# Six weight differences of each head on GpSimd, and VectorE's SBUF-SBUF operations in the three-operand form

## The reference

```
h    = rmsnorm(x, pre_w) * (1 + scale) + shift
proj = h @ w_in                              # q, k, v, z, b, a, rx, gate
# DeltaNet head: short conv, silu, l2norm; then per chunk and direction
tmat = strict_lower((k*beta) @ k.T * decay) + I
u, w = solve(tmat, [v*beta, k*beta*exp(g)])
v_new = u - w @ S;  o = (q*exp(g)) @ S + (q @ k.T * decay) @ v_new
S = S * gl + (k*exp(g_last - g)).T @ v_new
# RG-LRU block: gates r, i from x; a = exp(-8 r softplus(-lam))
h_t = a_t * h_{t-1} + sqrt(1 - a_t**2) * i_t * x_t      # both directions
y = x + gate * rmsnorm(concat(o * silu(z), h * silu(gate)) @ w_out, post_w)
```

## Time and profile before

| | |
|---|---|
| median of three runs | 1477.31 us (1476.23 to 1486.73) |
| the profiled execution | 1494.5 us |
| its span | 1492.9 us |
| mean granted clock of TensorE | 0.954 |
| busy: TensorE, VectorE, ScalarE, GpSimd | 1404.3, 1017.6, 751.4, 118.5 us |
| VectorE's differences of `w_in` (L1449) | 51, 68.2 us |
| heads 1 to 7 start their scans near | 374, 514, 653, 794, 933, 1077, 1219 us |

### The profile page before, as it was taken

One profiled execution on the slowest core, in us unless ns is written; L12 is line 12 of the kernel. 1 busy time (PEld: TensorE's weight loads), 2 busy tenths in 40 slices (PEclk: granted clock), 3 DMA queues, 4 the chain that ended last, 5 costly groups with the idle time before them and its releaser, 6 DMA issues.

```text
span 1492.9 us, 24459 instructions
## 1 busy us (share of the span) xinstructions
PE 1404.3 (94%) x8198; PEld 1256.5 (84%) x8198; DVE 1017.6 (68%) x2101; ACT 751.4 (50%) x1878; POOL 118.5 (8%) x144
## 2 busy tenths in 40 slices
PE   6899999999999899989999998999999987699997
PEld 3599989987998799889989997998899864488886
DVE  4775867786778778777976797878678845722222
ACT  3535474646465655666474647465646644411110
POOL 3001000100010000000000100010001000211211
PEclk9999989996999999999989999999699978699999
DMA  8221111111012111111111102012102350432440
GB/s 322 71 70 42 29 38 52 45 47 56 19 45 64 43 30 61 34 43 45 45 34 58 45 31 72 19 48 61 43 16 74 129 218 32 141 103 88 126 126 29
DMA packets 95203, 100.48 MB, mean 67 GB/s; under 512 B 4293, under 2 KB 81350, under 8 KB 94058
## 3 DMA queue, kind: packets, MB, share of 16 engines
q1 hardware_dynamic: 92138, 88.38, 19.2%
q0 software_dynamic: 2944, 10.49, 1.8%
HBM read 83.55 MB, written 15.30 MB: 66 GB/s over the span
## 4 chain that ended last, share of the span: by engine, by line
PE 83%; ACT 7%; issue 4%; DVE 4%; DMA 1%; SPq 0%; DVEq 0%; ACTq 0%
PE bank L722 14%; PE bank L720 14%; PE bank L721 14%; PE bank L1025 13%; PE bank L888 4%; PE bank L932 3%; PE bank L977 2%; PE bank L848 2%; PE bank L995 2%; PE bank L987 2%; PE bank L968 2%; PE bank L963 2%; PE bank L810 2%; ACT L1178 1%; PE bank L899 1%
## 5 line engine op out<-in xcount | busy, mean ns | idle before, releaser
L720 PE MATMUL bank<-hT_hi,w_hi 128*128 128x384 f32 (+1 forms) x1224 | 439.2, 359 | 3.4 <-DVE hT_lo L1477 3.4
L722 PE MATMUL bank<-hT_hi,w_lo 128*128 128x384 f32 (+1 forms) x1224 | 417.1, 341 | 0.0
L721 PE MATMUL bank<-hT_lo,w_hi 128*128 128x384 f32 (+1 forms) x1224 | 416.4, 340 | 0.0
L720 PEld LDWEIGHTS bank<-hT_hi,w_hi 128*128 128x128 f32 x1224 | 233.3, 191 | 7.5 <-issue 3.2
L721 PEld LDWEIGHTS bank<-hT_lo,w_hi 128*128 128x128 f32 x1224 | 233.5, 191 | 1.2
L722 PEld LDWEIGHTS bank<-hT_hi,w_lo 128*128 128x128 f32 x1224 | 232.4, 190 | 0.0
L1314 ACT ACTIVATE arena<-bank,arena 128x128 f32<-128x128 f32 x272 | 78.6, 369 | 185.8 <-PE bank L977 185.6
L1533 DVE SCALAR_TENSOR_TENSOR arena<-arena 128x1154 f32<-128x1154 f32 x96 | 135.9, 1416 | 3.5 <-DVE arena L1531 1.1
L1025 PE MATMUL bank<-wo_hi,ot_hi 128*128 128x512 f32 x288 | 114.6, 398 | 17.5 <-DVE ot_lo L1851 13.4
L1025 PE MATMUL bank<-wo_lo,ot_hi 128*128 128x512 f32 x288 | 113.9, 396 | 0.0
L1025 PE MATMUL bank<-wo_hi,ot_lo 128*128 128x512 f32 x288 | 113.9, 395 | 0.0
(11 more groups left out here) (233 smaller groups left out, 2394.0 us busy)
## 6 DMA issues: line engine op xcount, KB each, us to landing
w_raw<-w_in SPq DMA_DIRECT2D x51, 512.0 KB, 4.0
arena<-scr_G SPq DMA_DIRECT2D x16, 576.0 KB, 4.9
ot<-scr_o SPq DMA_DIRECT2D x9, 1024.0 KB, 6.7
arena<-x_sample SPq DMA_DIRECT2D x16, 512.0 KB, 7.6
arena<-ada_w SPq DMA_DIRECT2D x8, 1024.0 KB, 17.0
wo<-w_out SPq DMA_DIRECT2D x4, 2048.0 KB, 22.4
scr_o<-arena POOLq DMA_DIRECT2D x8, 576.0 KB, 3.1
scr_o<-arena POOLq DMA_DIRECT2D x8, 512.0 KB, 2.9
```

What stands on the lines that cost most here:

```text
L720: pe.matmul(out, w_hi[:, slot, k], hT_hi[:, k, cols], start=first, stop=False)
L721: pe.matmul(out, w_hi[:, slot, k], hT_lo[:, k, cols], start=False, stop=False)
L722: return pe.matmul(out, w_lo[:, slot, k], hT_hi[:, k, cols], start=False, stop=last)
```

## The change

All six differences of a head leave VectorE's list and are put into GpSimd's, as the same subtraction with the same semaphore. The six of the prologue stay with VectorE. In GpSimd's list numbers 4 and 5 stand behind the clearing of Zt, before the store of the head's output; number 6 stands behind that store; number 1 stands at the head of the loop's body, before the store of the states; numbers 2 and 3 stand behind the masks. Apart from that, VectorE's `tensor_tensor` operations whose two operands both lie in SBUF (in `rg_piece`, `norm_o` and the elimination) become `scalar_tensor_tensor` with a factor of 1.0, which computes (a * 1.0) op b.

```diff
@@ GpSimd @@
+            def low_w(slot, made):
+                gp.wait_ge(w_hi_made.sem, made)
+                gp.tensor_tensor(w_lo[:, slot], w_raw[:, slot], w_hi[:, slot].bitcast(F32), ALU.subtract)\
+                  .then_inc(w_lo_made.sem, 1)
+
             def phase_a(b):
...
                 gp.wait_ge(decay_exped.sem, decay_exped.next(b, INST))
                 own(gp.tensor_tensor(clear_mark, ident[:, 0:1], ident[:, 0:1], ALU.mult))
                 gp.memset(Zt, 0.0).then_inc(Zt_cleared.sem, 1)
+                low_w(1, w_lo_made.at(b, 4))
+                low_w(0, w_lo_made.at(b, 5))
...
             masks(-1)
             phase_a(-1)
+            low_w(1, w_lo_made.at(-1, 6))
             own.clear()
             with gp.Fori(0, HEADS - 1) as h:
+                low_w(0, w_lo_made.at(h, 1))
                 stores(h)
                 masks(h)
+                low_w(1, w_lo_made.at(h, 2))
+                low_w(0, w_lo_made.at(h, 3))
                 gp.wait_ge(stepped.sem, stepped.at(h, 18))
...
                 store_rg(h)
                 phase_a(h)
                 store_oz(h)
+                low_w(1, w_lo_made.at(h, 6))
@@ VectorE: the same form in "sum", "gate" and norm_o @@
-                    dve.tensor_tensor(RB, RB, RC, ALU.mult).then_inc(rg_bx_made.sem, 1)
+                    dve.scalar_tensor_tensor(RB, RB, 1.0, RC, ALU.mult, ALU.mult).then_inc(rg_bx_made.sem, 1)
@@ VectorE: phase_a @@
-                low_w(1, w_lo_made.at(b, 4))
                 own.settle()
...
-                low_w(0, w_lo_made.at(b, 5))
...
-                    if k == 10:
-                        low_w(1, w_lo_made.at(b, 6))
...
-                    own(dve.tensor_tensor(tmp, X[:, k + 1:, k:k + 1].to_broadcast([P, rows, k]),
-                                          X[:, k:k + 1, 0:k].to_broadcast([P, rows, k]), ALU.mult))
-                    own(dve.tensor_tensor(X[:, k + 1:, 0:k], X[:, k + 1:, 0:k], tmp, ALU.add))
+                    own(dve.scalar_tensor_tensor(tmp, X[:, k + 1:, k:k + 1].to_broadcast([P, rows, k]), 1.0,
+                                                 X[:, k:k + 1, 0:k].to_broadcast([P, rows, k]), ALU.mult, ALU.mult))
+                    own(dve.scalar_tensor_tensor(X[:, k + 1:, 0:k], X[:, k + 1:, 0:k], 1.0, tmp, ALU.mult, ALU.add))
@@ VectorE: joins and scan @@
-                    if slot == 10:
-                        low_w(0, w_lo_made.at(b, 1))
...
-                        if step == 1:
-                            low_w(1, w_lo_made.at(b, 2))
-                        if step == 7:
-                            low_w(0, w_lo_made.at(b, 3))
```

More of the change, by code:

```diff
@@ L1601, in rg_piece @@
                     dve.wait_ge(rg_scanned.sem, rg_scanned.at(b, 6))
-                    dve.tensor_tensor(RH, RH, RC, ALU.add).then_inc(rg_out_made.sem, 1)
+                    dve.scalar_tensor_tensor(RH, RH, 1.0, RC, ALU.mult, ALU.add).then_inc(rg_out_made.sem, 1)
                 else:
@@ L1605, in rg_piece @@
                     dve.wait_ge(silued.sem, silued.at(b, 2))
-                    dve.tensor_tensor(RH, RH, sg, ALU.mult).then_inc(rg_out_made.sem, 1)
+                    dve.scalar_tensor_tensor(RH, RH, 1.0, sg, ALU.mult, ALU.mult).then_inc(rg_out_made.sem, 1)
             def norm_o(b):
@@ L1610, in norm_o @@
                 own(dve.reciprocal(hcc["rstd"], hcc["rstd"]))
-                dve.tensor_tensor(o_tok, o_tok, hcc["rstd"].unsqueeze(2).to_broadcast([P, NCH, P]), ALU.mult)\
+                dve.scalar_tensor_tensor(o_tok, o_tok, 1.0, hcc["rstd"].unsqueeze(2).to_broadcast([P, NCH, P]), ALU.mult, ALU.mult)\
                    .then_inc(o_normed.sem, 1)
```

## The result

The changed kernel takes 1569.01 us (median of 4 runs, 1558.64 to 1570.97), the kernel before 1481.8 us beside it (4 runs, 1476.23 to 1486.73): ratio 1.0575, 95% interval 1.0507 to 1.0644, 87 us slower. The forecast was 1530 us with a range to 1552: the direction is right, the size is short by 39 us (52.7 us slower forecast, 87 measured). The profiled execution took 1567.3 us, span 1565.7 (before 1492.9), so the profiles differ by 72.8 us; before's own was 13 us above its median.

What follows compares the result with a forecast made beforehand. TensorE's projections were taken to set a head's length, VectorE ending slightly ahead. Stop 34.7, clock 16 and contention 2 sum to 52.7 us; added to the median 1477.3 this gave 1530 us, range 1504 to 1552.

Steps and rivals of the forecast that it cites:

- The stop at tile 3: TensorE waits at tile 3 for GpSimd's difference 4, behind the clearing: 4.4 us seven times, 3.9 once, 34.7 us.
- The clock behind the stops: After each TensorE stop the granted clock falls to half: 2.0 us times 8, 16 us, between 0 and 23.
- Rival (a): TensorE's stop at tile 3 alone, the clock does not fall for it: 1514 us, chance 0.26.
- Contention: GpSimd's differences hold VectorE's operations by the SBUF lock, mainly at the first convolution tap: 2 us, from 0 to 6.
- VectorE about 50 us less busy: Sign expected in the changed profile: VectorE about 50 us less busy, and idle longer before the joins.
- the elimination pairs at their old durations: Sign expected in the changed profile: VectorE's elimination pairs take as long as before.
- The form: VectorE's three-operand form costs the same as the two-operand one (1355 against 1361 ns at 128x1154): 0 us.
- Removed work: The differences leaving VectorE, 45 x 1.23 = 55 us less work there: a gain of 0, bound 8.6 us.
- Rival (b): GpSimd's difference 1 gets in between VectorE's two recurrence scans and holds the long one: 16 us more, 1546, chance 0.13.
- nothing downstream has time to give: the seam's slack is VectorE's, not TensorE's: Behind TensorE's stop every later reader follows TensorE; at the seam between heads VectorE idles 1.50 us before the joins.
- The range's upper end: 1552 us, from 40.7 for the stops, 23 for the clock, 6 for contention and 5 more: 75 us.

Runs made afterwards that it cites:

- e2: The kernel before with difference 4 alone moved to GpSimd, behind the clearing of Zt; VectorE waits for it before difference 5. Measured 1526.7 us, ratio 1.0319.
- e4: The changed kernel, but SyncE's load of the next head's tile 0 also waits for the head's last projection. Measured 1538.3 us, ratio 1.0417.
- e10: The changed kernel with difference 4 given back to VectorE at its old place. Measured 1479.7 us, ratio 1.0008.
- e1: The changed kernel; inside the loop GpSimd makes difference 4 before its wait for the decay's exponentials, prologue as in the change. Measured 1497.9 us, ratio 1.0122.
- e3: The kernel before with the three-operand form alone; all differences stay on VectorE. Measured 1479.7 us, ratio 1.0005.
- e5: The changed kernel with the two-operand form back in VectorE, so only the six differences move. Measured 1567.8 us, ratio 1.0591.
- e12: The kernel before plus a 512 KB DRAM copy that nobody waits for, issued behind each head's 17th projection. Measured 1515.3 us, ratio 1.0271.
- e8: The kernel before; the joins' first product waits for all eight placings of Zt instead of four. Measured 1534.8 us, ratio 1.0368.
- e7: The changed kernel with difference 1, within the joins, given back to VectorE at its old place. Measured 1569.2 us, ratio 1.0613.

## Why the prediction was short

**The stop at tile 3: right.** Forecast 4.4 us seven times and 3.9 once, 34.7; measured 4.15 to 4.3 each, 32.9 as a wait, 34.2 by stages. The difference of 128x1024 takes 2.34 us undisturbed, forecast 2.3.

**The clock behind the stops: right.** Forecast 16 us, measured 14.5; in e2 stop and clock together 50 against 50.7. Rival (a), the stop alone, is out.

**Contention: perhaps too small, and partly in the wrong place.** Forecast 2 us, bound 6. e4 holds everything of the change but the early load, and is 57 us over its before against e2's 50: 7 us for the holds by the medians, 14 by the ratios, 8.4 by the profiles (3.4 of it behind the stops, 4.9 in the scans). With intervals of plus or minus 12 us for e4 and 8 for e2 this may also be nothing. e10, which has the moves of all but difference 4, costs at most 5 us by its interval. VectorE gave back the 55 us it was relieved of and a little more: the normed output 14 us, elimination some 17, and the first taps 29, with a mean of 2035 ns instead of 813:

```profile
L1543 DVE TENSOR_SCALAR arena<-arena 128x1154 f32<-128x1154 f32 x24 | 48.9, 2035 | 6.2 <-ACT arena L1116 6.2
...
474.13 2.49 DVE L1687 SCALAR_TENSOR_TENSOR arena<-arena 128x240 f32<-128x240 f32 x1
```

The last is one product of the elimination, 0.41 us long when alone, beside difference 6. The forecasts "VectorE about 50 us less busy" and "the elimination pairs at their old durations" failed by this. It cost TensorE little because VectorE had time to give, as the prediction said, and e1 shows the price once it has none. The three-operand form is held like the other, as the prediction took from the Trainium skill (SBUF — State Buffer, Who interferes with whom).

**The form: right** (e3, e5). **Removed work: right**, worth nothing (e10). **Rival (b)**, the lock on the recurrence scan: did not occur; difference 1 issues behind the scans and waits itself (4.2 instead of 2.35 us).

**The step that failed** is "nothing downstream has time to give: the seam's slack is VectorE's, not TensorE's". The rows were read rightly, but VectorE's slack was taken as harmless. It had a reader: SyncE waits for VectorE's transposes before it loads the next head's states and tile. The stop (4.3 us) and the moved differences 5 and 6 gave VectorE 4.5 us of lead, the load moved 4.5 us forward and onto the packet with TensorE's next instructions; seams 7 us, joins 22 us by the profiles, 29.5 us by the medians of e5 and e4. The steps from before to e2, e4 and e5 are thus 50, 7 and 29.5 us. That they add up to the change's 87 is no check on them, since each step starts where the last ended; what shows the third step's mechanism is e4, which takes the early load away, and e12, which puts one in its place. The range's upper end had 5 us for a worse draw of the clock and nothing for this.

## What to carry to other kernels

Work placed behind a wait is priced from that wait's release, with all instructions in between and the clock's fall behind the stop. When an engine is relieved, list who waits for it, the queues that issue loads above all, and look at what their transfers will then run beside: here an instruction packet, at the turn of TensorE's loop. Work moved from VectorE to GpSimd may relieve VectorE by less than its length: here 55 us went and as much came back in operations held.

## What the hardware showed unexpectedly

- What is read here as TensorE's next block of instructions at the turn of its loop comes as one 16 KB packet. It starts 1.5 to 1.6 us before the last projection where no load is under way (before, e4; 1.0 to 1.2 in four seams of e3, e8 and e10, for no cause that was found), and 0.7 to 1.9 us later than that, by the trace's packets of all heads, where 512 KB are (changed, e12). The joins' first product follows its end by 1.70 to 1.87 us in these four kernels. How the packet is held, in a queue or at the memory, no run here tells.
- A seam of 2.5 to 3.1 us ahead of the joins instead of 1.1 to 1.7 was followed by 38 to 72 us more at half clock in the joins of eight heads (e12, e8 against before). Over all traces the five kernels with long seams have 79 to 144 us of half clock there, the nine others 9 to 72; e7 (79) and before (72) nearly meet, so the tie is one of many heads, not of each.
- GpSimd's difference was itself held beside VectorE's work: 4.2 to 4.4 us instead of 2.34 for number 1, issued into VectorE's scan in seven heads; mean 2.7 us over 45.
